# One tile further ahead in a gated linear attention stage: scores and decay gates moved forward, exponentials taken in two steps, decay logarithms split into two rounded parts

## The reference

```python
def gla_chunked(q, k, v, logg, s0, with_output=True):
    ...
    g = jnp.cumsum(logg.astype(f32).reshape(b, n, GLA_CHUNK, h, dk), axis=2)
    ...
    g_mid = g[:, :, GLA_CHUNK // 2 - 1][:, :, None]
    scores = jnp.einsum('bnihd,bnjhd->bnhij', q * jnp.exp(g - g_mid), k * jnp.exp(g_mid - g))
    mask = jnp.tril(jnp.ones((GLA_CHUNK, GLA_CHUNK), dtype=bool))
    scores = jnp.where(mask, scores, 0.0)
    o_intra = jnp.einsum('bnhij,bnjhv->bnihv', scores, v)
    o_inter = jnp.einsum('bnihd,nbhdv->bnihv', q * jnp.exp(g), s_start)
    return (o_intra + o_inter).reshape(b, l, h, dv), s_final
```

## Time and profile before

| | |
|---|---|
| Median of 3 runs | 1600.6 us (1597.98 to 1603.92) |
| The profiled execution | 1602.36 us, of which its span of instructions is 1600.6 us |
| PE busy | 1542.7 us, 96% of the span |
| Attention stage of layer 0 (dft end to last msq) | 264.2 to 311.1 us |
| Attention stage of layer 1 | 1128.2 to 1159.4 us |
| Share of PE in the chain that ended last | 89% |

### The profile page before, as it was taken

The page is one execution under the profiler, slowest core; times in us unless marked ns, Lnnn a source line. Parts: engine busy times, 40 slices in busy tenths (PEclk is TensorE's granted clock), DMA queues, the critical chain, the costliest instruction groups (busy, mean ns, idle before and its releaser), DMA issues.

```text
span 1600.6 us, 22917 instructions
## 1 busy us (share of the span) xinstructions
PE 1542.7 (96%) x9056; PEld 1388.6 (87%) x9056; DVE 855.1 (53%) x1316; ACT 569.0 (36%) x916; POOL 593.4 (37%) x309
## 2 busy tenths in 40 slices
PE   5999999999999999999999989999999999999997
PEld 2899999886799999999999868888898888888887
DVE  2576888637646425662366675477666332223237
ACT  4644214526444213441244255432535322222221
POOL 0532212245324524553255223332252444444441
PEclk9899999999999999999999999999999999999999
DMA  9544432355312203122121341563140333323221
GB/s 370 201 159 157 158 117 76 106 176 209 120 51 82 79 26 100 59 80 79 53 80 60 138 171 53 197 198 112 34 159 27 117 115 116 125 92 105 92 85 60
DMA packets 54062, 183.93 MB, mean 115 GB/s; under 512 B 5650, under 2 KB 10642, under 8 KB 51028
## 3 DMA queue, kind: packets, MB, share of 16 engines
q1 hardware_dynamic: 47826, 168.85, 31.2%
q10 hardware_dynamic: 6146, 13.83, 2.5%
HBM read 171.13 MB, written 11.53 MB: 114 GB/s over the span
## 4 chain that ended last, share of the span: by engine, by line
PE 89%; DVE 4%; ACT 3%; DMA 2%; POOL 1%; SPq 1%; issue 1%; ACTq 0%; DVEq 0%; POOLq 0%
PE A L1055 61%; PE A L1310 8%; PE N L1310 4%; PE G L1310 4%; PE A L1244 1%; PE A L1238 1%; PE G L1213 1%; DMA raw<-modw 1%; PE G L1365 1%; PE G L1172 1%; PE A L1206 1%; PE N L1226 1%; PE A L1252 1%; PE N L1156 1%; POOL w_lo L992 1%
## 5 line engine op out<-in xcount | busy, mean ns | idle before, releaser
L992 POOL TENSOR_TENSOR w_lo<-raw,w_hi 128x1024 fp32r<-128x1024 f32 (+2 forms) x163 | 385.8, 2369 | 662.0 <-ACT w_hi L1392 624.5
L1055 PE MATMUL A<-h_hi,w_hi 128*128 128x512 f32 (+2 forms) x1264 | 416.2, 360 | 21.7 <-POOL h_lo L1038 10.6
L1055 PE MATMUL A<-h_hi,w_lo 128*128 128x512 f32 (+2 forms) x1264 | 405.3, 351 | 0.0
L1055 PE MATMUL A<-h_lo,w_hi 128*128 128x512 f32 (+2 forms) x1264 | 405.1, 351 | 0.0
L1392 ACT ACTIVATE w_hi<-raw 128x1024 fp32r<-128x1024 f32 (+2 forms) x163 | 167.3, 1028 | 373.4 <-PE A L1055 332.7
L1055 PEld LDWEIGHTS A<-h_hi,w_hi 128*128 128x128 f32 x1264 | 236.0, 191 | 65.6 <-POOL h_lo L1038 16.3
L1055 PEld LDWEIGHTS A<-h_hi,w_lo 128*128 128x128 f32 x1264 | 237.7, 191 | 22.0
L1055 PEld LDWEIGHTS A<-h_lo,w_hi 128*128 128x128 f32 x1264 | 238.1, 191 | 21.2 <-issue 0.5
L1055 PE MATMUL A<-g_hi,w_hi 128*128 128x384 f32 (+2 forms) x480 | 146.8, 349 | 3.8 <-DVE g_lo L1883 2.0
L1055 PE MATMUL A<-g_lo,w_hi 128*128 128x384 f32 (+2 forms) x480 | 145.9, 347 | 0.0
L1055 PE MATMUL A<-g_hi,w_lo 128*128 128x384 f32 (+2 forms) x480 | 145.8, 347 | 0.0
(11 more groups left out here) (313 smaller groups left out, 2643.5 us busy)
## 6 DMA issues: line engine op xcount, KB each, us to landing
raw<-stream SPq DMA_DIRECT2D x150, 512.0 KB, 3.7
mraw<-modv SPq DMA_DIRECT2D x54, 512.0 KB, 4.2
mraw<-modw SPq DMA_DIRECT2D x10, 1024.0 KB, 6.7
raw<-pairs SPq DMA_DIRECT2D x18, 512.0 KB, 4.7
raw<-modw SPq DMA_DIRECT2D x6, 1024.0 KB, 14.7
x<-x_keep ACTq DMA_DIRECT2D x4, 1536.0 KB, 13.5
raw<-stream SPq DMA_DIRECT2D x16, 384.0 KB, 3.1
bg<-modv SPq DMA_DIRECT2D x10, 512.0 KB, 4.1
```

What stands on the lines that cost most here:

```text
L992: pool.tensor_tensor(lo, like_chunk(n, raw[:, n % RAW, 0:WIDTH[n]]), hi.bitcast(F32), ALU.subtract).then_inc(lo_done, 1)
L1055: m = pe.matmul(dst[:, at:at + t1 - t0], a, b[:, k, t0:t1], start=(first and p == 0), stop=(last and p == 2))
```

## The change

Four things change, all in the attention.

1. **Order.** Two gates and the first score move in between the dft steps, and every later score and gate stand one tile further ahead. One tile's steps are now score(a+1), gate(a+2), msq(a-1), o(a).
2. **Exponentials in two steps.** For tiles 2 and on, ACT takes the two exponentials for the scores in the gate step (now after `score` of tile a-2 and not after its `o`) and the third only in the `o` step of the tile two before. DVE's multiplication with `qT` is cut in the same way: 512 elements in the gate step, and 512 more in `state_part`, which waits for the third exponentials and stands in the `o` step. PE's `o` waits for it (`qs_ready`).
3. **Split decay logarithms.** `ls` of one tile is rounded by ACT into `ls_high` (one 128x512 copy a tile), POOL subtracts to get `ls_low` (one 128x512 subtraction a tile), and the constant matrix is rounded once (`mat_r`). The gate product becomes two fp32r matmuls where one fp32 matmul stood. There is one buffer each of `ls_high` and `ls_low`, so the next tile's parts are only made when ACT has seen the gate of the tile before.
4. The new tiles lie where `wd`, the first part of `mat` and `mrow` lie.

```diff
         for s4 in range(5 if L == 0 else 4):
+            if s4 == 2:
+                for g in (0, 1):
+                    order.append(("gate", L, tiles[1], g))
+                order.append(("score", L, tiles[0]))
             order.append(("dft", L, s4))
+        order.append(("halves", L))
         for a, tt in enumerate(tiles):
-            order.append(("score", L, tt))
-            if a == 0:
-                order.append(("halves", L))
             if a + 1 < len(tiles):
+                order.append(("score", L, tiles[a + 1]))
+            if a + 2 < len(tiles):
                 for g in (0, 1):
-                    order.append(("gate", L, tiles[a + 1], g))
+                    order.append(("gate", L, tiles[a + 2], g))
...
+                if e[0] == "gate":
+                    tiles = tiles_of(e[1])
+                    at = tiles.index(e[2])
+                    if at == 0 and e[3] == 0:
+                        low_until(PLAN.n0[e] + RING)
+                    elif e[3] and at:
+                        low_until(max(done[0], PLAN.n0[("wout", e[1])] + max(0, at - 3)))
+                    if at + e[3] < len(tiles) and (e[3] or at == 0):
+                        pool.wait_ge(lshi_ready, nth(e[1], tiles[at + e[3]]) + 1)
+                        pool.tensor_tensor(ls_low[:, :], ls[:, tiles[at + e[3]], :], ls_high[:, :].bitcast(F32),
+                                           ALU.subtract).then_inc(lslo_ready, 1)
...
-                    read_out(pe, ("z", L, tt))
+                    pe.wait_ge(lslo_ready, nth(L, tt) + 1)
                     for pr in range(2):
-                        m = pe.matmul(G[g][:, pr * 256:(pr + 1) * 256], ls[:, tt, g * KW + pr * P:g * KW + (pr + 1) * P],
-                                      mat[:, g * 256:(g + 1) * 256], start=True, stop=True)
+                        own = slice(g * KW + pr * P, g * KW + (pr + 1) * P)
+                        pe.matmul(G[g][:, pr * 256:(pr + 1) * 256], ls_high[:, own], mat_r[:, g * 256:(g + 1) * 256],
+                                  start=True, stop=False)
+                        m = pe.matmul(G[g][:, pr * 256:(pr + 1) * 256], ls_low[:, own], mat_r[:, g * 256:(g + 1) * 256],
+                                      start=False, stop=True)
...
+                    pe.wait_ge(qs_ready, nth(L, tt) + 1)
...
                     if nth(L, tt) - 6 * L >= 2:
-                        act.wait_ge(full["o"], 6 * L + tiles_of(L).index(tt) - 1)
+                        act.wait_ge(full["score"], 6 * L + tiles_of(L).index(tt) - 1)
...
                     act.activation(E[:, b, 0, g, :, :], src[:, :, 1, :], ACT.Exp)
-                    act.activation(E[:, b, 2, g, :, :], src[:, :, 1, :], ACT.Exp, scale=-1.0)
-                    m = act.activation(E[:, b, 1, g, :, :], src[:, :, 0, :], ACT.Exp)
-                    m.then_inc(free[f"G{g}"], 1)
+                    m = act.activation(E[:, b, 2, g, :, :], src[:, :, 1, :], ACT.Exp, scale=-1.0)
+                    m.then_inc(exp_ready, 1)
+                    if nth(L, tt) - 6 * L < 2:
+                        act.activation(E[:, b, 1, g, :, :], src[:, :, 0, :], ACT.Exp).then_inc(free[f"G{g}"], 1)
+                    at = tiles_of(L).index(tt) + 1
+                    if g and at < len(tiles_of(L)):
+                        act.activation(ls_high[:, :], ls[:, tiles_of(L)[at], :], ACT.Copy).then_inc(lshi_ready, 1)
                 elif kind == "o":
                     b = turn(L, e[2])
                     act.wait_ge(full["o"], PLAN.full[e])
+                    if tiles_of(L).index(e[2]) + 2 < len(tiles_of(L)):
+                        for g in range(2):
+                            src = G[g][:, :].rearrange("p (r w t) -> p r w t", r=2, w=2)
+                            act.activation(E[:, b, 1, g, :, :], src[:, :, 0, :], ACT.Exp).then_inc(free[f"G{g}"], 1)
...
+            def state_part(L, tt):
+
+                for g in range(2):
+                    read_out(dve, ("gate", L, tt, g))
+                own = E[:, turn(L, tt), 1, :, :, :]
+                q = qT[:, :, tt * P:(tt + 1) * P].rearrange("p (o r) t -> p o r t", o=1).to_broadcast([P, 2, 2, P])
+                dve.tensor_tensor(own, own, q, ALU.mult).then_inc(qs_ready, 1)
```

More of the change, by code:

```diff
@@ L560, in bass_hybrid_block @@
         par = sb("par", [P, DEPTH * PCOLS + 16])
+        ls_low_t, mat_t, ls_high_t = ExitStack(), ExitStack(), ExitStack()
+        with ls_low_t:
+            ls_low = sb("ls_low", [P, 512], F32R, stack=ls_low_t)
         wd = sb("wd", [97, 512])
         mask = sb("mask", [P, 2, P], I32)
+        with mat_t:
+            mat_r = sb("mat_r", [P, 4 * P], F32R, stack=mat_t)
         mat = sb("mat", [P, 4 * P + 2 * P + 2])
@@ L577, in bass_hybrid_block @@
         mraw = sb("mraw", [P, 2, MW])
+        with ls_high_t:
+            ls_high = sb("ls_high", [P, 512], F32R, stack=ls_high_t)
         mrow = sb("mrow", [P, 512])
@@ L673, in bass_hybrid_block @@
         qk_ready, r_scaled = sem("qk_ready"), sem("r_scaled")
+        lshi_ready, lslo_ready = sem("lshi_ready"), sem("lslo_ready")
+        exp_ready, qs_ready = sem("exp_ready"), sem("qs_ready")
         osq_ready, orstd_ready, yg_ready, yhi_ready, ylo_ready = (
@@ L1554, in _ @@
                     tt = e[2]
+                    if nth(L, tt) == 0:
+                        act.wait_ge(consts_in, 16 * 4)
+                        link(act.activation(mat_r[:, :], mat[:, 0:4 * P], ACT.Copy))
+                    if tt == tiles_of(L)[0]:
+                        for t in tiles_of(L):
+                            read_out(act, ("z", L, t))
+                        act.activation(ls_high[:, :], ls[:, tt, :], ACT.Copy).then_inc(lshi_ready, 1)
                     act.wait_ge(full["four"], PLAN.full[e])
```

12 lines of the change are left out of this document (8 added, 4 removed).

## The result

| | before | changed |
|---|---|---|
| Median | 1599.6 us (18 runs, 1596.7 to 1603.9) | 1603.4 us (18 runs, 1600.8 to 1605.4) |
| Ratio, 95% interval | | 1.0020 (1.0012 to 1.0028) |
| The profiled execution | 1602.4 us, span 1600.6 | 1600.8 us, span 1599.0 |

The change costs 3.2 us by the ratio, 3.8 by the medians, where 6.25 were forecast: the sign holds and so does the mechanism within the two stages, but the size is about half. The two profiled executions even stand the other way round, the changed one 1.6 us shorter: before's was among its slowest, after's was the fastest of its 18. So the traces are compared stage by stage and not by their ends.

What follows compares the result with a forecast made beforehand. The prediction took PE to bound the kernel, with DVE and ACT only 0.25 us a tile behind. Layer 0's +4.75 us and layer 1's +1.5 gave +6.25, so 1600.6 us becomes 1606.9, range 1594 to 1614.

Steps and rivals of the forecast that it cites:

- the layout: Each engine's attention instructions laid out in sequence, DVE products and POOL subtractions taking turns; doubled ls_low subtractions: +7.5 us.
- (1): Layer 0, first dft: it comes 0.87 us earlier but DVE's last Fourier split does not, +0.6 us.
- (2): Layer 0, first scores: score(0) waits for its kT product behind DVE and POOL work, +1.4 us; score(1) +0.2.
- (3): Layer 0, before score(3): DVE's fold, queued behind state_part of tile 2, delays the products, +3.1 us.
- (4): Layer 0, later gates: PE waits for the cycle through ACT, DVE and POOL, 2.2 + 0.9, +3.1 us.
- (5): Layer 0, stage end: no score covers the last three msq, square behind third exponentials, 1.4 + 0.7 + 0.7 = +2.8 us.
- The waits of layer 1: Layer 1: first gates 0.95 us, gate(1) 0.6, score(1) 2.0, msq(1) 1.85, last two msq 0.7 each.
- the second rival: PE's clock also halves after waits in layer 0's attention: +9.3 us, 1609.9 us, 1614 if in both layers; 18 in 100.
- the ring: Attention cycle over ACT, DVE and POOL between h_hi copies: 7.54 us before, forecast 9.1 with ls_low, 7.8 without.
- PE did not stay the bound: Rival for the attention: PE stays the bound, only gates and old waits count, -9.8 us, 1590.8 us; 7 in 100.
- Hinder each other little: Rival for the attention: DVE and POOL instructions need not take turns, -2.0 us, 1598.6 us; 18 in 100.
- The dearer subtractions: Rival for the attention: POOL's subtractions need 1.8 us each, +10 us, 1610.6 us; 5 in 100.

Runs made afterwards that it cites:

- fold first: Changed kernel with DVE's part of the fold moved right behind the second half of the Fourier result: 1601.9 us, ratio 1.0006.
- the filler: Changed kernel with 16 matmuls of constants put into PE's wait before score(3) of layer 0: 1604.5 us, ratio 1.0032.
- the four edits: Changed kernel with DVE's fold early, last third exponentials behind the square, layer 0's score(0) one dft step later, last o before the preceding tile's msq: 1606.2 us.
- small `ls_low`: Changed kernel with POOL's subtraction to ls_low cut from 512 to 4 columns from each layer's third tile on: 1602.0 us, ratio 1.0013.
- double `ls_low`: Changed kernel with every POOL subtraction to ls_low made twice, one behind the other: 1609.9 us, ratio 1.0061.
- the three edits: Changed kernel with DVE's fold early, last third exponentials behind the square, layer 0's score(0) one dft step later: 1599.0 us, ratio 1.0008.
- both kernels with `ls_low` on DVE: The three edits and the split alone, each with DVE making the ls_low subtraction from a layer's third tile on: 1596.5 and 1598.3 us.
- the split alone: Kernel before, its order and exponentials kept, with only the split decay logarithms (ls_high, ls_low, mat_r) added: 1603.9 us, ratio 1.0017.

## Why the size was wrong

**The gates.** Forecast -0.87 us a tile, measured 1.83 - 1.06 = 0.77. The new matmuls stand 0.12 apart as read from the earlier trace rows, but the first of each gate takes 0.22.

**ls_high and ls_low, and the turns of DVE and POOL.** Right: moving POOL's subtractions to DVE gives back 2 and 4 us in the stages, cutting them short 2.5 to 2.9. Doubling them costs 4.6 to 5.0, less than the layout's 7.5, so the layout prices added turns too high. The rule of the Trainium skill cited in the prediction (SBUF — State Buffer, section "SBUF: two separate sides") agrees with these rows, the undisturbed 0.68 us of the product that reads PSUM included.

**The waits of layer 0.** (1) 0.6 against 0.55. (2) 1.4 against 1.04, and 0.2 before score(1) against none. (3) 3.1 against 2.69; the fold began at 274.49, behind o(0), and `fold first` took 1.8 of this wait away. (4) 3.1 against 0.42 + 0.83 in the trace with the slow stretch, and 1.10 + 0.33 + 1.01 = 2.44 where the filler kept the clock up. (5) 2.8 against 1.23 + 0.70 + 0.70. Stage: +4.75 against +4.5 and +4.9. The agreement is in part luck: the waits come to 8.2 us where 11.2 were forecast, and that is made up by gates that save 0.6 less, by the slow stretch itself, in which PE's work took longer, and by the overlap that each wait breaks.

**The waits of layer 1.** 0.95 against 0.55 and a second one of about 0.3; 0.6 against 0.51; 2.0 against 1.28; 1.85 against 1.77; 1.4 against 1.4. Stage: +1.5 against +1.5.

**The step that failed** is the one from the stages to the whole: "Nothing behind the attention takes this up, since PE is the path there too". The stages cost the 6.0 us that were forecast, and the kernel lost 3.2. One microsecond of the distance between 1606.9 and 1603.4 is the base: the median of before over three runs, 1600.6, came out at 1599.6 over 18. Most of the rest is TensorE's clock, and it is the second rival turned round. The clock did fall behind the wait before score(3), as that rival said. But it cost nothing there, because the ring and not PE set the pace: with 0 (the filler), 3.4 and 6.8 us of it both stages together take 109.5, 109.5 and 109.9 us.

What the program takes outside the stages follows the half-clock time there. Over 13 traces it is 1481.6 us and 0.39 for each us at half the clock, within 1.1 us (both counted within the span of instructions); the fourteenth, the four edits, lies 3.3 above, its waits behind the stages. So the time outside has no other part that the change moved by more than about 1 us. The first trace of before has 39.4 us at half the clock outside the stages, that of the changed kernel 22.2, and so they stand the other way round. The second ones have 28.9 and 28.7, and there the changed kernel is 5.3 us longer with stages that are 6.4 longer: the cost of the stages arrives nearly whole.

In the executions it does not, since their mean clock is the same as before's on the same chip (0.98973 and 0.98971). With 3.4 to 6.8 us of slow time in the stage, where it is free, as much less of it is left for the places where it costs, and at 0.39 each that is an estimated 1.3 to 2.7 us of the 2.5 that are missing. The filler fits: the stage lost its slow stretch, its mean clock is not above that of before's runs beside it, and the kernel came out 1.6 us slower at like clock with a stage of equal length.

What is shown is that the slow time in the stage is free and that the mean clock of the changed kernel is not lower. That slow time is moved and not added rests on this kernel's two traces and the filler, and it is no rule: in the fold first, the small and the double `ls_low` and the three edits the mean clock lies 0.0006 to 0.0015 under that of before's runs beside them, so there the slow time in the stage seems to have been added, in part or whole. A difference of two such means is itself uncertain by 0.0005 to 0.0007, 1.6 to 2.2 us at half the clock, so the runs don't settle this for any single kernel. The table takes a loss of clock out, and so it cannot tell the two apart. In its "rest" the six traces with slow time in the stage have -2.7 in the mean, the six without -0.7 (the four edits with their waits of 3.4 us taken off). That difference of 2.0 is about what the free stretches explain: they are 5.1 us in the mean, 0.0016 of mean clock, 1.8 us by the line through before's runs (an estimate). The -0.7 stays open; the unchanged kernel's -0.5 is nearly as much.

Why the later stretches get shorter isn't known. One of them can be seen in the windows of the changed kernel, 420.30 to 423.60, which answer to the second of the earlier trace rows: 3.3 us where before has 6.2. In the double `ls_low` it is absent, in `fold first` and the small `ls_low` it has its full length, and it is short in the filler and in both kernels with `ls_low` on DVE too, so this stretch alone does not balance the account.

**The rivals.** PE did not stay the bound: the ring is at 7.56 and 8.64 us where it decides at 6.92. "Hinder each other little" is refuted by the split alone (stages +4.75, where -5.7 was its forecast), by both kernels with `ls_low` on DVE and by the rows themselves. The dearer subtractions: a subtraction alone takes 1.26 us, and 1.4 to 2.2 where DVE has the turn first; that is the turn and not an own price.

## What to carry to other kernels

When an engine's work is cut in a stage where a ring over other engines has 3% to spare, the ring has to be shortened first; here the split lengthened it (from 7.54 us a turn to 9.51 in the split alone), the new order left it at 7.55 and cost in other places, and each alone cost the kernel as much as both. Before giving a spare engine new work, look at whose instructions it stands beside: 0.68 us more on DVE was cheaper than 1.3 us on a POOL that was idle otherwise. And a sum over a stage becomes the kernel's only at equal clock: set the mean clock of many executions beside it, and look behind the stage too, since what is taken out of its end can come back in front of the next.

## What the hardware showed unexpectedly

- A DVE product of two SBUF tiles (128x512, alone 0.68 us) that begins while a POOL subtraction runs ends about 0.55 us after it, and so takes up to 2.4 us. POOL's 128x512, begun behind such a product, takes 1.4 to 2.2 instead of 1.26, and its 128x1024 2.81 instead of 2.36. The DVE product with one operand in PSUM keeps its 0.68 us in the middle of a POOL instruction, and so do the masked copies from PSUM (1.35 for two).
- Slow stretches of TensorE are not a fixed loss. Over 106 runs of one kernel the mean clock lies at 0.990, single executions between 0.987 and 0.994, and this scatter explains 78% of the variance of the times. The fastest two and the slowest two of 12 runs differ by 7 us.
